# Two-layer decoder trunk on one core: the twelve S3 differences of its three layer changes, on VectorE behind S4 instead of on GpSimd between the weight operations

## The reference, cut to what matters

```python
for i in range(2):
    y = rms_norm(h, norm_mix[i])
    y = gla_mixer(y, ...) if i == 0 else gmlp_mixer(y, ...)   # gated linear attention, then gMLP
    h = h + y
    h = h + (silu(z @ w_gate[i]) * (z @ w_up[i])) @ w_down[i]  # z = rms_norm(h, norm_ffn[i])
return rms_norm(h, norm_final)
```

## Time and profile before

| | |
|---|---|
| median of three runs | 2605.78 us |
| the profiled execution | 2604.42 us |
| its span, first to last instruction | 2602.6 us |
| TensorE matmuls busy | 2530.8 us, 97% |
| VectorE busy | 1726.5 us, 66% |
| GpSimd busy | 1289.8 us, 50% |
| ScalarE busy | 1105.8 us, 42% |
| mean granted TensorE clock | 0.993 |

### The profile page before, as it was taken

One profiled execution on the slowest core, in us unless ns is written; L12 is line 12 of the kernel. 1 busy time (PEld: TensorE's weight loads), 2 busy tenths in 40 slices (PEclk: granted clock), 3 DMA queues, 4 the chain that ended last, 5 costly groups with the idle time before them and its releaser, 6 DMA issues.

```text
span 2602.6 us, 33638 instructions
## 1 busy us (share of the span) xinstructions
PE 2530.8 (97%) x11752; PEld 2094.0 (80%) x11752; DVE 1726.5 (66%) x2209; ACT 1105.8 (42%) x1952; POOL 1289.8 (50%) x985
## 2 busy tenths in 40 slices
PE   7998999989999999999999999999998999999998
PEld 6787887868888888887888888888877888888886
DVE  4224657877777866576675899965667778556556
ACT  4124776453333344454333433344534333334444
POOL 2134445545555555445666455545445555555543
PEclk9999999999999999999999999999999999999999
DMA  5673233516666648664888455587633566325764
GB/s 196 212 263 130 65 94 125 178 53 202 219 213 212 226 150 298 192 209 146 276 295 266 138 182 182 172 301 255 207 105 114 198 214 218 125 78 191 278 194 146
DMA packets 305517, 489.30 MB, mean 188 GB/s; under 512 B 32274, under 2 KB 128147, under 8 KB 305364
## 3 DMA queue, kind: packets, MB, share of 16 engines
q1 hardware_dynamic: 305364, 487.32, 55.9%
HBM read 326.15 MB, written 152.70 MB: 184 GB/s over the span
## 4 chain that ended last, share of the span: by engine, by line
PE 87%; DVE 5%; ACT 3%; issue 2%; DMA 1%; POOL 0%; SPq 0%; DVEq 0%; ACTq 0%
PE ps L617 27%; PE ps L619 27%; PE ps L618 27%; PE ps L2567 2%; DVE r_all L1758 1%; PE ps L2426 1%; DVE r_all L1783 1%; DMA resid_scratch<-r_all 1%; PE ps L2354 1%; PE ps L2397 1%; DVE n_all L1796 1%; PE ps L2404 0%; PE ps L2263 0%; DVE xl_all L1765 0%; ACT ebuf L1334 0%
## 5 line engine op out<-in xcount | busy, mean ns | idle before, releaser
L685 POOL TENSOR_TENSOR ring_lo<-stg,ring_hi 128x512 fp32r<-128x512 f32 x682 | 974.6, 1432 | 933.1 <-ACT ring_hi L681 932.5
L681 ACT ACTIVATE ring_hi<-stg 128x512 fp32r<-128x512 f32 x682 | 429.3, 631 | 1041.8 <-PE ps L619 978.6
L617 PE MATMUL ps<-xh_all,ring_hi 128*128 128x512 f32 x1568 | 615.9, 393 | 10.4 <-issue 5.7
L618 PE MATMUL ps<-xl_all,ring_hi 128*128 128x512 f32 x1568 | 611.7, 390 | 0.0
L619 PE MATMUL ps<-xh_all,ring_lo 128*128 128x512 f32 x1568 | 611.7, 390 | 0.0
L703 DVE TENSOR_TENSOR s_ring<-s_stage,s_ring 128x512 fp32r<-128x512 f32 x242 | 303.6, 1267 | 226.5 <-ACT s_ring L699 225.9
L617 PE MATMUL ps<-ring_hi,s_ring 128*128 128x512 f32 x1064 | 415.7, 391 | 3.8 <-DVE r_all L1783 2.6
L619 PE MATMUL ps<-ring_hi,s_ring 128*128 128x512 f32 x1064 | 414.1, 389 | 0.0
L618 PE MATMUL ps<-ring_lo,s_ring 128*128 128x512 f32 x1064 | 414.0, 389 | 0.0
L617 PEld LDWEIGHTS ps<-xh_all,ring_hi 128*128 128x128 f32 x1568 | 295.5, 188 | 73.0 <-issue 9.2
L619 PEld LDWEIGHTS ps<-xh_all,ring_lo 128*128 128x128 f32 x1568 | 295.2, 188 | 61.8
(11 more groups left out here) (227 smaller groups left out, 3551.7 us busy)
## 6 DMA issues: line engine op xcount, KB each, us to landing
s_stage<-h_scratch SPq DMA_DIRECT2D x238, 256.0 KB, 3.5
stg<-t_scratch SPq DMA_DIRECT2D x200, 256.0 KB, 3.0
h_scratch<-r_all SPq DMA_DIRECT2D x34, 1024.0 KB, 5.1
h_scratch<-r_all SPq DMA_DIRECT2D x80, 256.0 KB, 3.1
stg<-in_w_ffn_gate SPq DMA_DIRECT2D x34, 512.0 KB, 4.5
stg<-in_w_ffn_up SPq DMA_DIRECT2D x34, 512.0 KB, 5.9
stg<-in_w_ffn_down SPq DMA_DIRECT2D x66, 256.0 KB, 3.5
t_scratch<-r_all SPq DMA_DIRECT2D x28, 512.0 KB, 2.9
```

Of the source, the lines that this page charges most:

```text
L617: pe.matmul(bank, s_hi, m_hi, start=first, stop=False, skip_group_check=more)
L618: pe.matmul(bank, s_hi, m_lo, start=False, stop=False, skip_group_check=more)
L681: nc.scalar.activation(weight_slot(ring_hi, g), weights(g), ACT.Copy).then_inc(wh_done, 1)
L685: nc.gpsimd.tensor_tensor(weight_slot(ring_lo, g), weights(g), f32(weight_slot(ring_hi, g)), ALU.subtract).then_inc(wl_done, 1)
```

## The change

The function `sum3` moves from GpSimd's program to VectorE's, and loses its wait for `sum1_done`. `head_sums` and its call between GpSimd's weight differences go. VectorE makes the four S3 tiles in a row: in "v" at the end of `head`, behind the last S4 tile; in "f0" and "f1" behind the low halves 8 to 11. Ahead of the four stands one wait for `sum2_done`, which has been reached by then. Nothing else changes: same arithmetic, same tiles, no DMA moved or added.

```diff
@@ GpSimd @@
-            def sum3(n, i):
-
-                pool.wait_ge(sum1_done, 4 * n + i + 1)
-                nc.gpsimd.tensor_tensor(r_all[:, 8 + 2 * i, :], r_all[:, 2 * i, :], r_all[:, 8 + 2 * i, :],
-                                        ALU.subtract).then_inc(sum3_done, 1)
-
-            def head_sums(n, i):
-
-                if i in (0, 1, 3, 4):
-                    sum3(n, (0, 1, 3, 4).index(i))
...
-                if name in ("f0", "v", "f1"):
-                    head_sums(("f0", "v", "f1").index(name), i)
@@ VectorE @@
+            def sum3(n, i):
+
+                nc.vector.tensor_tensor(r_all[:, 8 + 2 * i, :], r_all[:, 2 * i, :], r_all[:, 8 + 2 * i, :],
+                                        ALU.subtract).then_inc(sum3_done, 1)
...
                 if kind is not None:
                     sum4(n, kind, 3)
+                if kind == "V":
+                    dve.wait_ge(sum2_done, 4 * n + 4)
+                    for i in range(4):
+                        sum3(n, i)
...
                             head(n, "U")
                             for r in range(8, 12):
                                 turned_lo(n, "U", r)
+                            dve.wait_ge(sum2_done, 4 * n + 4)
+                            for t in range(4):
+                                sum3(n, t)
```

## The result

| | before | after |
|---|---|---|
| median of 9 runs each, same session (us) | 2605.78 (2604.4 to 2609.26) | 2614.93 (2610.9 to 2615.91) |
| profiled execution (us) | 2604.4 | 2615.34 |
| its span (us) | 2602.6 | 2613.4 |
| granted TensorE clock, mean | 0.993 | 0.991 |

The ratio (after over before) is 1.003, with an interval of 1.0019 to 1.004: the changed kernel is slower by 5 to 10 us. The medians lie 9.2 us apart where 6.9 us were forecast.

What follows compares the result with a forecast made beforehand. TensorE's matmuls were taken to bound the kernel. A 5.3 us stop in the second head plus 1.6 us of slow clock, 6.9 us on the 2605.8 us median, gave 2612.7 us; whole range 2606.5 to 2616.8 us.

Steps and rivals of the forecast that it cites:

- The stop of 5.3 us: Second head: TensorE stands still behind P5, as r = 12 waits for a low half behind four S3; 5.3 us.
- The upper bound of 7.9 us: Second head: four S3 that each wait for a whole GpSimd instruction take 7.9 us, a stall of 7.5 us.
- The price of one turn on the port: Second head: VectorE and GpSimd alternate, about 1.7 us a pair; three S3 so, the fourth 0.6 us, 5.7 us together.
- The clock, 1.6 us: Behind the new stop in the second head TensorE runs at clock 0.50: 1.6 us lost, bounds 0 and 3.5 us.
- First and third head, 0: "f0" and "f1": S3 run at 0.6 us each while GpSimd has no work; cost 0, or 0.3 us.
- the sum of 6.9 us: Whole kernel: 5.3 us of stop plus 1.6 us of slow clock make it 6.9 us slower.
- The pause without the slow clock: Rival: the second head's stop leaves TensorE's clock alone, 5.3 us slower, 2611.1 us; chance 0.20.
- S3 finds the port free: Rival: in the second head GpSimd doesn't take turns with S3; stall 2.0 us, 2607.8 us; chance 0.10.
- S3 meets GpSimd in "f0" and "f1": Rival: first and third head's four S3 take 6.7 us beside GpSimd, transposes 16 and 17 wait; about 2617.5 us; chance 0.05.
- The relief reaches the chain: Rival: GpSimd's emptied places in first and third head free VectorE's last-tile chain, 4 us earlier; 2598.3 us; chance 0.05.

Runs made afterwards that it cites:

- experiment 1: Changed kernel with the four S3 of "v" moved behind low halves 13 to 15: 2607.79 us, ratio 1.0001 to the kernel before.
- experiment 2: Changed kernel with S3 on VectorE only in "v", back on GpSimd in "f0" and "f1": 2612.72 us, ratio 1.0019 to the kernel before.
- Experiment 3: Changed kernel with S3 on VectorE only in "f0" and "f1", back on GpSimd in "v": 2607.70 us, ratio 1.0000 to the kernel before.
- experiment 8: Kernel before, S3 left on GpSimd, with GpSimd waiting at step 0 of "f0" and "f1" for the fourth S4: 2598.95 us, ratio 0.9969.
- the repeat: The changed kernel run again without an edit: 2613.14 us, ratio 1.002 to the kernel before.
- Experiment 6: Changed kernel with TensorE's transposes of r = 11 in "v" repeated nine times to fill the stop: 2610.61 us, ratio 1.0014 to the kernel before.
- experiment 5: Changed kernel with two S3 of "v" early and two behind low halves 13 to 15: 2609.03 us, ratio 1.0004 to the kernel before.
- Experiment 7: Changed kernel with S3 of "v" behind low halves 13 to 15 and GpSimd in "f0", "f1" waiting for the fourth S4: 2605.15 us, ratio 0.9993.
- experiment 4: Changed kernel with TensorE's transposes of r = 12 behind P6 instead of P5: 2609.99 us, ratio 1.001 to the kernel before.

## Why the prediction was right, point by point

**The stop of 5.3 us (forecast as "the second head, where the cost is"): right, term by term.** The profile of the changed kernel starts its second head 4.69 us later than that of before (P2 at 1196.47 against 1191.78). With that shift taken off, S3 starts at 1206.27 (forecast 1206.3), the low half of r = 8 at 1211.94 (1212.0) and r = 12 at 1212.76 (1212.8). The four S3 took 5.74 us (5.7). The six weight differences end at 1209.19 (1209.2), the next at 1210.86 (1210.9), so three S3 had a partner, as argued. The upper bound of 7.9 us gave a partner to all four; with three it is 3 x 1.97 + 0.69 = 6.6 us, and the measured time still lies below it. From low half to transposes it was 1217.45 - 1216.63 = 0.82 us, the value borrowed from the first head. r = 12 came 5.25 to 5.30 us later than before in every profile with four S3 in that place (20.96 to 21.01 against 15.71), and 2.98 us later with two. What the prediction had otherwise is how much of this TensorE stands still: it gave all 5.3 us, by a P4 at full clock, and the row shows 3.54 us, because P4 was 1.57 us slower and used up part of the wait. Experiments 1, 2 and 3 show that this head holds the whole loss and that the order makes it.

**The price of one turn on the port: right.** The trace decided between two prices: a pair took 1.7 us, and four S3 5.74 us, not the 7.9 us that come from waiting for GpSimd's whole instruction each time. The Trainium skill (SBUF — State Buffer, "Who interferes with whom") says that issue order decides who blocks. The trace of the kernel before agrees. GpSimd's weight difference of 1198.90 was first and took 1.27 us; VectorE's normalisation came second and took 2.07 us, where it takes 1.28 us with GpSimd held back (experiment 8, third head):

```profile
1199.18 2.07 DVE L1758 SCALAR_TENSOR_TENSOR r_all<-r_all,stats,gain_bc 128x1024 f32<-128x1024 f32 x1 [0.68 <-DMA resid_scratch<-r_all]
```

The differences of the same chain take 0.69 us in experiment 8 and 1.65 us without the wait. The runs also agree with that section's sentence that a VectorE instruction with at most one SBUF input, outside its two-port modes, does not contend: the three low halves at 1208.08 in experiment 1 take 1.87 us, 0.6 us each, beside GpSimd.

**The clock, 1.6 us: the size right, the reason only half.** Behind the stop the clock was 0.50 for 2.95 us (forecast: about 3 us). Transposes and P6 lost 0.49 + 1.05 = 1.5 us by their durations (0.49 + 1.04 in the repeat, and P6 alone 1.58 us in experiment 2); from r = 12 to P8 it is 6.70 - 5.27 = 1.4 us. Experiment 6 shows it as a term of its own, in one profile. What did not hold is the sentence that behind a pause of 2.60 us in the second head the clock is still 1.00. That was one execution. Of the twelve profiles, P4 behind that same pause ran at full clock in four (2.99 to 3.00 us) and at a reduced one in eight (4.32 to 4.57 us), with the change and without. Where it is slow, the kernel without the stop loses 24.3 - 22.96 = 1.3 us too, while with the stop this is absorbed by the wait. So the edit costs 6.7 us against a fast P4 and 29.67 - 24.3 = 5.4 us against a slow one. With eight of twelve slow I estimate 5.8 us in the mean. All five profiles with four S3 early had a slow P4; that a fast one would meet the same r = 12 is argued from experiment 5 and not shown for four. The three comparisons with four S3 early in "v" (1.003, 1.002, 1.0019) average 1.0023, or 6.0 us. The 9.2 us between the first medians stand above this, with an interval of 5 to 10 us that holds it. In the two profiles of that comparison 3.8 us come from the later start and 1.0 us from the clock in the first head, and neither is a term of the prediction. So the sum of 6.9 us lies a little above the best estimate of the effect and below the first medians.

**First and third head, 0: right, with one argument too weak.** With the shift of 3.79 us taken off, S3 starts at 553.65 in the first head (forecast 553.7), the second group of low halves ends at 557.34 (557.3), and the weight sums end at 558.53 (558.6), 0.68 us each. Experiment 3 gives 1.0000. But the prediction held a late weight sum for harmless because P10 is five products off. Experiment 7 shows that it need not be: ScalarE waits for it in order, the high halves of the next transposes stand behind, and TensorE stops. In the changed kernel it did no harm because the first weight sum ended at 561.72 us, half a microsecond before ScalarE's high half for P10 at 562.23 us, which waited for TensorE.

**The rivals.** *The pause without the slow clock* fell: P6 took 4.03 to 4.57 us behind the stops of 3.54, 3.55, 3.75 and 2.82 us (the changed kernel twice, experiments 2 and 5); behind the 1.04 us of experiment 4 the clock was 1.00. *S3 finds the port free* fell: 5.74 us, with GpSimd's row showing its partners. *S3 meets GpSimd in "f0" and "f1"* did not happen in the changed kernel, but experiment 7 shows it as real once GpSimd is late: 5.09 and 5.88 us, where 6.7 us had been given. *The relief reaches the chain* fell for the reason given, the weight differences fill the places (x6 back to back). That the port holds the chain up was right all the same: with GpSimd held off, experiment 8 ran in 2598.95 us. That this is so near the 2598.3 us of the rival is partly luck. The rival emptied only the two places of S3 in each head, for 4 us, and added up to 3.5 us of clock, 7.5 us in all. Experiment 8 held back the weight differences too: P4 came 2.9 and 3.9 us earlier, and against the kernel before on the same chip the gain was 9.1 us (5 to 11). What gives that time is the emptiness and not the move of S3.

## What to carry to other kernels

An operation moved to a faster engine is priced by what stands behind it in that engine's queue: twelve differences that run in 0.68 us instead of 1.72 us made this kernel 0.2 to 0.3% slower, because four of them stood ahead of the one low half that TensorE needed next. What hangs on an instruction goes further than its own reader: a late operand also holds up everything behind the engine that waits for it in order. Taking work from a neighbour that shares the port does not empty the port while that neighbour has other work ready; if a chain matters, hold the neighbour back for its length by a wait (here 0.3% faster), and see what the work held back will meet next. Before a profile's pause is used as a price for the clock, look at it in several executions.

## What the runs showed of the hardware that I had not expected

- The same pause of 2.6 us left TensorE at full clock in four of twelve profiles and at a reduced one in eight, in kernels that do nearly the same work up to there, the changed kernel's profiles among the eight and the kernel's before among the four. In some of the eight the first matmul behind it already takes 0.77 us (experiments 2 and 8 are two), in another (the changed kernel again) the first takes 0.47 us and the change to 0.63 us a matmul comes about a microsecond later, where 0.39 us is usual at full clock. Why one execution goes one way and the next the other, no run here tells.
- With transposes repeated through the stop the clock was 1.00 in it and behind it: 3.93 us of matmuls in 4.20 us, and P6 in 3.00 us (experiment 6, one profile).
- The start of the program differs by up to 4.2 us between executions (P0 of the first head at 534.22 to 538.41 us), most of the 5.4 to 6.7 us that the edit costs. A difference between two spans has to be taken from marks inside the stage and not from the whole.
